# The first block's output and down products, and the norms behind them, in halves of 128 tokens; part of the output product between the steps of the delta rule

## What is computed

```
h   = rms_norm(x, mix_pre_norm)
mix = concat(sliding attention, block attention, gated delta rule) @ w_out    # 256 x 1024
x   = x + rms_norm(mix, mix_post_norm)
h   = rms_norm(x, ffn_pre_norm)
x   = x + rms_norm(glu_ffn(h), ffn_post_norm)     # 1024 -> 2 x 2816, conv over 3 tokens, 2816 -> 1024
```

## Time and profile before

| what | value |
|---|---|
| median of three runs | 1840.1 us |
| span of the profiled execution | 1836.4 us |
| profiled execution's own time | not listed apart; the median lies 3.7 us over the span |
| PE, DVE, ACT busy | 94%, 39%, 32% of the span |
| mean granted TensorE clock | 0.968 of full speed |
| first block's stages in the span | delta rule's levels 133 to 157 us, w_out and norms 166 to 219, w_up 219 to 357, w_down 357 to 434, norms 434 to 461 |

### The profile page before, as it was taken

The page is one execution under the profiler, slowest core; times in us unless marked ns, Lnnn a source line. Parts: engine busy times, 40 slices in busy tenths (PEclk is TensorE's granted clock), DMA queues, the critical chain, the costliest instruction groups (busy, mean ns, idle before and its releaser), DMA issues.

```text
span 1836.4 us, 21251 instructions
## 1 busy us (share of the span) xinstructions
PE 1727.3 (94%) x8462; PEld 996.2 (54%) x8462; DVE 709.1 (39%) x1365; ACT 586.1 (32%) x1025; POOL 31.8 (2%) x58
## 2 busy tenths in 40 slices
PE   9998999999999999999999999898999889998898
PEld 8877788887878787787623222232232322232232
DVE  2584466603769999951222111121111211122112
ACT  1153122202356564650133322223222322223222
POOL 4000000000000000100000000000000000000000
PEclk9999999999999999999999999989999999899999
DMA  5330244442443443266779999999999999999996
GB/s 185 116 135 27 80 147 160 154 158 101 171 158 138 141 159 143 92 265 245 314 292 434 428 432 426 429 434 426 433 430 427 430 429 432 428 433 429 430 428 287
DMA packets 36015, 523.47 MB, mean 285 GB/s; under 512 B 3992, under 2 KB 4184, under 8 KB 5336
## 3 DMA queue, kind: packets, MB, share of 16 engines
q1 hardware_dynamic: 34704, 511.75, 68.1%
q10 hardware_dynamic: 1224, 10.50, 1.6%
HBM read 521.12 MB, written 1.12 MB: 284 GB/s over the span
## 4 chain that ended last, share of the span: by engine, by line
PE 48%; DMA 33%; DVE 13%; DVEq 3%; ACT 2%; issue 1%; ACTq 0%; SPq 0%
DMA arena<-in_experts 32%; PE psum L577 10%; PE psum L1172 8%; PE psum L1144 7%; PE psum L923 6%; PE psum L896 4%; DVE arena L2052 4%; PE psum L1005 3%; DVE arena L2040 2%; PE psum L1154 2%; DVEq L2054 1%; PE psum L661 1%; PE psum L640 1%; PE psum L876 1%; DMA arena<-in_panels 1%
## 5 line engine op out<-in xcount | busy, mean ns | idle before, releaser
L1172 PE MATMUL psum<-arena 128*34 128x512 f32 x2048 | 466.9, 608 | 54.4 <-DMA arena<-in_experts 32.2
L1172 PEld LDWEIGHTS psum<-arena 128*34 128x34 f32 x2048 | 135.9, 113 | 358.3 <-issue 319.6
L923 PE MATMUL psum<-arena 128*128 128x272 f32 x1344 | 315.6, 394 | 1.6 <-DVE arena L2260 1.6
L1679 DVE SCALAR_TENSOR_TENSOR arena<-psum,arena 34x512 f32<-34x512 f32 x64 | 44.2, 690 | 691.7 <-ACT arena L1242 691.7
L923 PEld LDWEIGHTS psum<-arena 128*128 128x128 f32 x1344 | 255.4, 191 | 57.1 <-DVE arena L2260 2.1
L1144 PE MATMUL psum<-arena 128*34 128x512 f32 x1024 | 251.2, 647 | 11.0 <-DMA arena<-in_experts 10.0
L577 PE MATMUL psum<-arena 128*128 128x256 f32 x992 | 215.4, 378 | 0.0
L577 PEld LDWEIGHTS psum<-arena 128*128 128x128 f32 x992 | 187.2, 189 | 27.6 <-issue 1.2
L1144 PEld LDWEIGHTS psum<-arena 128*34 128x34 f32 x1024 | 65.9, 120 | 184.1 <-issue 180.3
L1642 ACT ACTIVATE arena<-psum 34x512 f32<-34x512 f32 x64 | 38.0, 594 | 323.0 <-PE psum L1172 323.0
L2052 DVE SCALAR_TENSOR_TENSOR arena<-arena 128x272 f32<-128x272 f32 x240 | 112.1, 528 | 3.5
(11 more groups left out here) (425 smaller groups left out, 1434.5 us busy)
## 6 DMA issues: line engine op xcount, KB each, us to landing
arena<-in_experts SPq DMA_DIRECT2D x56, 4096.0 KB, 41.4
arena<-in_experts SPq DMA_DIRECT2D x80, 2048.0 KB, 41.7
arena<-in_panels SPq DMA_DIRECT2D x91, 1024.0 KB, 4.8
arena<-in_down_panels SPq DMA_DIRECT2D x8, 1408.0 KB, 6.2
arena<-scr ACTq DMA_DIRECT2D x4, 2176.0 KB, 9.4
out<-arena SPq DMA_DIRECT2D x4, 256.0 KB, 2.0
arena<-in_x_cols ACTq DMA_DIRECT2D x1, 548.0 KB, 5.2
arena<-in_x_cols SPq DMA_DIRECT2D x1, 544.0 KB, 4.7
```

Of the source, the lines that this page charges most:

```text
L923: ins = mm(pair[k][:, b, 0:T], slot8[k][:, c, b * P:(b + 1) * P], src[:, c, :], start=c == 0, stop=c == DC - 1)
L1172: ins = mm(psum[lo:lo + CAP, p % 2, :], xg[:, c, :], r_up[t % RING][:, c, :], start=c == 0, stop=c == DC - 1)
```

## The change

1. **Fill.** The attention rows of w_out (c = 0..3 of all four panels, 32 products) become `fill(count)`. 11 of them are issued ahead of the six levels (3, 2, 3, 1, 1, 1), 2 behind the levels, 2 ahead of the wait for vn1_ready, 4 between the two head sums and 13 behind them. Panels 2 and 3 (`more`) are loaded ahead of panels 0 and 1. Each panel's results now lie in one PSUM bank, a column range for each block.
2. **Halves.** The head norm, its gating, and the rest of w_out run for tokens 0 to 127 and then 128 to 255, with 128 columns in each product. ACT takes each half out while PE does the other (`take_panel`). The post norm's sum, its scale, the residual and the next norm's sum and scale are made for each half. The sums of squares are first added up on DVE (`add_half`), so that two products of ones are left of each.
3. **w_up.** The first two panels have buffers of their own (`up8`), loaded during the delta rule, and are multiplied in halves. Their undivided features are divided on DVE by `divided`, in the place of eight separate operations.
4. **w_down.** The first half of the hidden features is as before. The second half of the hidden features is done for the two token halves in turn, and two of its panels have buffers of their own (`down_more`). The second residual goes by halves as the first (halves of 144 and 128 columns where the meta tokens are along). `dt_rows` now stands behind both panels, not between them.
5. The wT and st1 products behind the levels change places, and so do their copies.

The core of the diff, without the lines removed (they are in the listing above):

```
--- before.py
+++ after.py
+            sp.wait_ge(ev("aT_ready"), 2)
+            sp.dma_start(up8[0].rearrange("p c n -> p (c n)"), a["panels"][PANELS["w_up"]]).then_inc(ev("up_loaded"), 16)
+            sp.wait_ge(ev("sz_ready"), after["sz_ready"] + 1)
+            sp.dma_start(up8[1].rearrange("p c n -> p (c n)"), a["panels"][PANELS["w_up"] + 1]).then_inc(ev("up2_loaded"), 16)
+            panels(PANELS["w_up"] + 2, 20)
+            sp.wait_ge(ev("mix_done"), after["mix_done"] + 6)
...
+            def sum_half(bank, name, count, cols):
+                pe.wait_ge(ev("add_" + name), after["add_" + name] + count)
+                for c in range(2):
+                    ins = mm(bank[:, cols], ones, sq[:, c, cols], start=c == 0, stop=c == 1)
+                ins.then_inc(ev("sum_" + name), 1)
+            def half_panel(k, weights, raw, cols, half, u_count, between=None):
+                for c in range(DC):
+                    pe.wait_ge(ev("u_ready"), u_count + c + 1)
+                    for b in range(2):
+                        ins = mm(pair[k][:, b, cols], weights[:, c, b * P:(b + 1) * P], raw[:, c, cols],
+                                 start=half == 0 and c == 0, stop=c == DC - 1, skip_group_check=True)
+                    if c == 3 and between:
+                        between()
...
+                    mm(mix_bank(0, i)[:, b * S:(b + 1) * S], w_out8[i][:, c, b * P:(b + 1) * P], mixed[:, c, :],
+                       start=b == 0 and c == 0, stop=False, skip_group_check=True)
+                filled[0] += count
...
+                fill((3, 2, 3, 1, 1, 1)[lv])
...
+            def head_sums(ck):
+                pe.wait_ge(ev("sq_ready"), SQ["o"] + ck + 1)
+                mm(use(3 - ck, "ro_ln", ck + 1), ones, sq_dn[:, ck * 512:(ck + 1) * 512],
                    start=True, stop=True).then_inc(ev("ro_sum"), 1)
+            head_sums(0)
+            fill(4)
+            head_sums(1)
+            fill(32 - filled[0])
+            assert filled[0] == 32
+            sums = [use(b, "rs_mix", b + 1) for b in range(2)]
+            for half in range(2):
+                pe.wait_ge(ev("mixed_ready"), half + 1)
+                for i in range(4):
+                    if half:
+                        pe.wait_ge(ev("mT_ready"), after["mT_ready"] + i + 1)
+                    for b in range(2):
+                        for c in range(4, DC):
+                            ins = mm(mix_half(0, i, half)[:, b, :], w_out8[i][:, c, b * P:(b + 1) * P], mixed[:, c, HALF[half]],
+                                     start=False, stop=c == DC - 1, skip_group_check=True)
+                    ins.then_inc(panel_done[(n[0] + i) % 2] if half and i < 2 else ev("mix_done"), 1)
+                    if half and i == 0:
+                        sum_half(sums[0], "mix", 1, mix_cols(0, 0))
+            n[0] += 2
+            def split_panels(stage, weights, raw, u_count, banks):
+                cols = [h_half(stage, half) for half in range(2)]
+                for at in range(2):
+                    k = (at + 1) % 2
+                    if stage == 0:
+                        loaded = ("up_loaded", "up2_loaded")[at]
+                        pe.wait_ge(ev(loaded), after[loaded] + 16)
+                        pe.wait_ge(ev("mT_ready"), after["mT_ready"] + 6 + 2 * at)
+                    else:
+                        pe.wait_ge(slot_loaded[k], 16 * ((n[0] + at) // 2 + 1))
+                        pe.wait_ge(copied[k], (n[0] + at) // 2)
+                    between = (lambda: sum_half(banks[1], "mix", 2 * stage + 2, mix_cols(stage, 1))) if at == 0 else None
+                    half_panel(k, weights[at], raw, cols[0], 0, u_count, between)
+                sum_half(banks[2], "h", 2 * stage + 1, cols[0])
+                for at in range(2):
+                    k = (at + 1) % 2
+                    ins = half_panel(k, weights[at], raw, cols[1], 1, u_count + DC)
+                    ins.then_inc(ev("up_done") if stage == 0 else panel_done[k], 1)
+                    if at == 0:
+                        sum_half(banks[3], "h", 2 * stage + 2, cols[1])
...
+            split_panels(0, up8, raw_h, 2 * DC, sums + [use(2, "rs_h", 1), use(3, "rs_h", 2)])
...
+            split_panels(1, [slot8[1], slot8[0]], raw_h1, 6 * DC, [psum[:, 0, :], psum[:, 1, :], G[0], G[2]])
+            dt_rows()
+            n[0] += 2
+            pe.wait_ge(ev("u_ready"), 9 * DC)
...
+            def take_panel(stage, half, i):
+                dst, name = ((mT, "mix_post"), (fT, "ffn_post"))[stage]
+                if half and i < 2:
+                    at = n[0] + i - 2 * stage
+                    act.wait_ge(panel_done[at % 2], at // 2 + 1)
                 else:
+                    act.wait_ge(ev("mix_done"), after["mix_done"] + 6 * stage + (3 if half else 1) + i)
+                part = mix_half(stage, i, half)
+                A(sq[:, 2 * i:2 * i + 2, mix_cols(stage, half)], part, ACT.Square).then_inc(ev("sq_mix"), 1)
                 for b in range(2):
+                    ins = A(dst[:, 2 * i + b, HALF[half]], part[:, b, :], ACT.Copy, scale=pcol(name, 2 * i + b))
+                ins.then_inc(ev("mT_ready"), 1)
...
+            def post_norms(stage, banks):
                 for i in range(4):
+                    take_panel(stage, 0, i)
+                half_scale(rs_at(stage, 0), banks[0], mix_cols(stage, 0), "mix", 2 * stage + 1)
+                take_panel(stage, 1, 0)
+                take_panel(stage, 1, 1)
+                square_part(stage, 0, 0)
+                take_panel(stage, 1, 2)
+                square_part(stage, 0, 1)
+                square_part(stage, 0, 2)
+                take_panel(stage, 1, 3)
+                square_part(stage, 0, 3)
+                half_scale(rs_at(stage, 1), banks[1], mix_cols(stage, 1), "mix", 2 * stage + 2)
+                if stage:
+                    act.drain()
+                    act.nop().then_inc(copied[0], 3)
+                half_scale(rs[:, h_half(stage, 0)], banks[2], h_half(stage, 0), "h", 2 * stage + 1)
+                for i in range(4):
+                    square_part(stage, 1, i)
+                half_scale(rs[:, h_half(stage, 1)], banks[3], h_half(stage, 1), "h", 2 * stage + 2)
+            post_norms(0, G)
...
+            def residual_part(stage, half, i, raw, gains):
+                part, hp = (mT, fT)[stage][:, 2 * i:2 * i + 2, HALF[half]], hT[:, 2 * i:2 * i + 2, META + P * half:META + P * half + P]
+                if i == 0:
+                    dve.wait_ge(ev("rs_mix"), after["rs_mix"] + 2 * stage + half + 1)
+                TT(part, part, rs_at(stage, half).unsqueeze(1).to_broadcast([P, 2, P]), MUL)
+                dve.drain()
+                TT(hp, hp, part, ADD).then_inc(ev(("res_ready", "h1_ready")[stage]), 1)
+                dve.drain()
+                lo = META * (stage == 0 or half)
+                for c in range(2 * i, 2 * i + 2):
+                    TS(raw[:, c, h_half(stage, half)], hT[:, c, lo + P * half:META + P * half + P], pcol(gains, c),
+                       None, MUL).then_inc(ev("u_ready"), 1)
+            def divided(stage, half, raw):
+                cols = h_half(stage, half)
+                dve.wait_ge(ev("rs_h"), after["rs_h"] + 2 * stage + half + 1)
+                TT(uT[:, :, cols], raw[:, :, cols], rs[:, cols].unsqueeze(1).to_broadcast([P, DC, cols.stop - cols.start]),
+                   MUL).then_inc(ev("u_ready"), DC)
+            def post_norms(stage, raw, gains):
+                add_half("mix", 8 * stage, mix_cols(stage, 0))
                 for i in range(4):
+                    residual_part(stage, 0, i, raw, gains)
+                    if i in (1, 2):
+                        add_half("mix", 8 * stage + 4, mix_cols(stage, 1), range(i, i + 1))
+                add_half("mix", 8 * stage + 4, mix_cols(stage, 1), range(3, 4))
+                add_half("h", 8 * stage, h_half(stage, 0))
+                for i in range(4):
+                    residual_part(stage, 1, i, raw, gains)
+                if stage == 0:
+                    divided(stage, 0, raw)
+                add_half("h", 8 * stage + 4, h_half(stage, 1))
+            post_norms(0, raw_h, "ffn_pre")
+            divided(0, 1, raw_h)
```

More of the change, by code:

```diff
@@ L265, in two_blocks @@
         gx, ux, fg, fe = [cut(2, S) for _ in range(4)]
+        rs_f = cut(S)
+        top[0] = max(top[0], up_end)
+        down_more = [cut(11 * PW) for _ in range(2)]
+        down11 = [t.rearrange("p (c n) -> p c n", c=11) for t in down_more]
         top[0] = mark1
@@ L827, in _ @@
             ins.then_inc(ev("st1_done"), 1)
+            bank = use(2, "wT_copied", 1)
+            for h in range(4):
+                ins = mm(bank[:, h * P:(h + 1) * P], kbg[:, h, :], XTf[1][:, h, :], start=True, stop=True)
+            ins.then_inc(ev("wT_done"), 1)
             bank = use(0, "o_copied", 1)
@@ L880, in _ @@
                 ins.then_inc(panel_done[k], 1)
                 n[0] += 1
[L882 to L893 removed]
```

(8 more changed lines are left out.)

364 lines of the change are left out of this document (156 added, 208 removed).

## The result

The changed kernel takes 1831.95 us (median of 4 runs, 1829.77 to 1832.45), the kernel before 1839.54 us (4 runs, the three known ones and one more, 1838.67 to 1840.18). The ratio is 0.9955 with a 95% interval of 0.9942 to 0.9968: 0.45% faster. The gain is 7.6 us (the profiled spans differ by 8.3), where 16.1 us were forecast, and the time lies 0.95 us above the upper end of the range. The time of a run lay 1.7 or 1.8 us over its span wherever both are known, so the profiled execution of before took about 1838.1 us and not its median. That bears on the level that I took for the sum, not on the gain.

A forecast was written before the change was run, and what follows sets the result against it. PE was taken to bound the kernel (48% of the span, expert weight fetches 33%). Gains of 13.0 and 3.5 us less 0.4 made 16.1, span 1820.3, time 1824.0 us; likeliest 1821 to 1827, with rivals 1819 to 1831.

The forecast's parts named there:

- the sum: Whole kernel: 16.1 us gained, span 1820.3, plus 3.7 us by which the median lies over the span, 1824.0 us.
- Output product and first norms: Last head output to third w_up panel: 40.3 us instead of 53.3, 13.0 less, at full clock with a 0.85 us wait.
- the meetings: First norms' new pipeline: four points where engines wait for each other's halves, with slack of 0 to 1.5 us.
- Delta rule: The six levels: fills mostly hidden in PE's idle gaps, sticking out 0.11 us in levels 3 to 5; +0.4 us.
- w_down and the second norms: w_down's start to the second block's next panel: 98.0 us instead of 104.0, no waits, 6.0 us gained for PE.
- What is given back: Around meta_rows: DVE's string starts no earlier, PE waits 2.0 us, then another 0.5; of 6.0 us gained 3.5 are left.
- rival 1: First norms: longer waits in the new pipeline, perhaps with the low clock; gain 9 to 13, 1827 to 1831 us; chance 0.2.
- The range's low-clock case: New pipeline, within rival 1: one gap brings the low clock again, costing 2.0 us more (4.64 against 2.6).
- It arrives at the end: From the second block on: the experts' loads wait for PE, so what is gained early should arrive at the end.
- Rival 2: Around meta_rows: the convolution string is not late, so all 6 us stay; 1819 to 1821 us; chance 0.1.
- Rival 3: The 368 products of 128 or 144 columns: they cost more than priced; at 0.32 us each, 1860 us; chance 0.04.

The follow-up runs named there:

- e5: The changed kernel with no fill ahead of levels 3 to 5, the three products going behind the second head sum; 1829.13 us, one run.
- e1: The changed kernel with the two down_more loads issued ahead of the 20 w_up panels; 1829.65 us, one run.
- e2: The changed kernel with the first token half of w_down taking its panels in the order 2, 3, 0, 1; 1829.03 us, one run.
- e8: The changed kernel with down_more loaded ahead of w_up's panels and w_down's first token half in order 2, 3, 0, 1; 1828.92 us, ratio 0.9941 to before.
- b3: The same kernel as e3, run once more; median 1827.43 us, ratio 0.9942 to the kernel before.
- e3: The changed kernel with dt_rows moved back between the two half passes of the second panel pair; median 1827.57 us, ratio 0.9932 to the kernel before.
- e6: The changed kernel with down_more loaded earlier, w_down's first token half in order 2, 3, 0, 1, and dt_rows between the half passes; 1821.45 us, ratio 0.9894.
- b6: The same kernel as e6, run once more; median 1823.42 us, ratio 0.9917 to the kernel before.
- e7: The kernel before with only dt_rows moved behind the second panel; median 1844.63 us, ratio 1.0023 to the kernel before.

## Why the prediction was right in its direction and wrong in its size

Point by point, by its own steps:

- **Output product and first norms** (13.0): right. From the last head output to the third w_up panel were 40.7 us where 40.3 were forecast, at a clock of 1.00, with one wait of 0.81 us (0.85) at the place named. The 80 records of L902 in the first piece of the chain took 8.93 us, 0.2233 us a product against the price of 0.2225.

```profile
164.70 0.47 PE psum L879 x2
...
175.81 8.93 PE psum L902 x80
...
207.46 2.59 PE psum L610 x12
```

- A residual part took 187.43 - 186.01 = 1.42 us (1.41), so the meetings held as worked out:

```profile
186.01 0.43 DVE L2035 TENSOR_TENSOR arena<-arena 128x256 f32<-128x256 f32 x1 [2.17 <-ACT arena L1460]
...
187.43 0.42 DVE L2035 TENSOR_TENSOR arena<-arena 128x256 f32<-128x256 f32 x1
```

- **Delta rule** (-0.4): mis-sized. Levels 3 to 5 lost 0.32 us each, 0.96 in all. I priced a fill at 0.433 us, as if products of another shape around it made no difference (e5).
- **w_down and the second norms** (6.0, "No waits are in it"): the work was right, the waits were missed. From w_down's start to the next panel were 99.95 us; less the wait of 1.43 that is 98.5, where 98.0 were forecast. But the wait of 1.43 us is there, and another of 1.44 ahead of w_down's start, 2.9 us together (e1, e2, e8). The step that failed is the sentence on the loads: "issued 20 us and more before use; the one queue behind SP's new waits is w_up's next panel". It looked at when the new buffers' own loads are needed. It did not ask what stands behind them in the queues: w_down's first panels do, and `down_more` was issued only 6.4 us ahead of them. Nor did it ask how long a slot's load has when the panels before it last half as long.
- **What is given back** (2.5): mis-sized, and this is the largest error. The wait was there, at its place, 1.55 us long (2.0). What followed was priced at 0.5 us and took 5.0: with 10.2 us at half speed, PE lost 2.3 us in `meta_rows` (6.5 against 4.2) and 2.7 in the panels (32.40 against 29.73). The whole is 14.3 - 7.6 = 6.7 us where 2.5 stood. b3 and e3 show that without the wait ACT's copy is 4.8 and 6.65 us earlier, e6 and b6 the same against e8 (6.6 and 6.7), and e7 shows a price of 4.8 us in the kernel before. The profile of before had the warning: the clock of 0.50 behind the first norms' wait. I used it in rival 1 for the new pipeline, where it did not come, and against the wait of 2.0 us in `meta_rows` I priced only its length. The same profile had the other case too: the wait of 2.56 us in the second norms (at 437.57), with a clock of 1.00 throughout. So a wait's length alone could not have told. The range's low-clock case was 2.0 us, from the earlier trace rows; here it was 5.0.
- **It arrives at the end**: right. At ACT's copy 7.6 us are left, at the end of the span 8.3. e6 and b6 show the same: 17.5 earlier than before at the copy, 15.3 to 15.8 in the span, less by no more than the spread of single executions.

Put together, in us: 16.1 forecast, less 4.2 around `meta_rows`, 2.9 for the transfers, 0.6 in the levels, 0.4 in the first norms and 0.5 in w_down's work makes 7.5, and 7.6 were measured. (In the running account the levels and first norms show only 0.7 of their 1.0, since the first level began 0.3 us earlier in the profiled run, at 132.44 against 132.74 in the earlier trace rows.)

Of the rivals, the first came nearest in size (1827 to 1831), but its mechanism did not occur: the meetings in the first norms kept to their times. The low clock that it speaks of came behind `meta_rows`. Rival 2 did not happen: DVE's string started when `dt_rows` ended. Rival 3 is excluded by the price of 0.2233 us. The Trainium skill, "TensorE: Matmul & The Clock Gate", section "Back-to-back issue gap", gives about 81 ns for a product of 128 columns with its weight load and about 56 ns without, a factor of 1.45. By that rule the 368 products would have cost 37 us more, an estimate from that page, and the trace does not agree: the 88 in w_down behind its wait took 19.76 us (391.75 to 411.51), 0.2245 each.

The 0.4 us in the first norms and the 0.5 us in w_down's work were not traced further. What also stays open is why an execution without a wait had 3.4 us of low clock in one case and none in another (b3 and e3 are the same kernel), why the two waits of 2.5 us in the kernel before were not alike, and whether a filler of another size would take the stretch away altogether.

## What to carry to other kernels

Price a new wait on TensorE with the clock that may come behind it, not with its length alone: here 1.55 us of idle time ahead of a run of small products cost 6.7 us. Taking the wait away paid, and so did filling it with useless products (2.1 us at ACT's copy). When products are halved, go through every load queue again: a buffer's load then has half the time, and a prefetch that is put ahead of another load delays that one. Keep the product that feeds a long string on another engine as early as it can stand, even where this breaks up an even run.

## What the runs showed of the hardware

- The low clock came in stretches of 3.4, 6.8 or 10.2 us between 445 and 495 us, in every kernel that had it: 6.8 or 10.2 where PE had waited 1.55 to 1.94 us (seven executions), none or 3.4 where it had not (six, before among them).
- Neither a wait nor its length decided it alone. The waits of 1.44 and 1.43 us in w_down stand between products with 128 rows of weights and 128 or 256 columns, and the clock stayed at 1.00 behind both. The wait of 1.55 us stands ahead of `meta_rows`, 16 small products. But small products are not needed for it: in the kernel before, the wait of 2.54 us in the first norms was followed by 3.4 us at the low clock and the wait of 2.56 us in the second norms by none, both ahead of full-sized products, and e7 shows the same pair. What decides is open. The Trainium skill, "TensorE: Matmul & The Clock Gate", section "HAM oscillation — how this bites in real kernels", describes a kernel whose waits for loads, of about 3 to 5 us, throw the clock back each time; in these runs the two waits for loads were shorter (1.44 and 1.43 us) and did not, and a wait hardly longer than these, with small products behind it, did.
- In the tail (900 to 1800 us) the low clock came to 82 to 99 us, and differed between executions of one kernel: 85.4 us in e3 and 98.9 in b3, with spans of 1821.9 and 1825.7 us. That goes with the spread of 2 us to either side, which limits what such a time can tell; that it is its cause was not tried.
- One product of 128x128 weights and 256 columns between two runs of 64x64 products of 64 columns took 0.63 us in place of 0.433, at full clock: 0.2 us for the two changes. The Trainium skill, "TensorE: Matmul & The Clock Gate", section "Step-by-step: what each phase is for", says that a weight load is pulled ahead of running products where the row groups don't conflict or the spare weight buffer takes it. No run here shows whether the load is what sticks out.
